# A hybrid decoder step in float32: which expert's down projection is kept in on-chip memory ahead of the weight stream, expert 7's or expert 31's

## The reference

```python
def hier_moe(t, w_route_group, w_route_expert, w_gate_up, w_down):
    ...
    out = jnp.zeros(t.shape, f32)
    for g in range(N_EXPERT_GROUPS):
        gu = jnp.einsum('td,edf->tef', t, w_gate_up[g])
        act = jax.nn.silu(gu[..., :D_EXPERT].astype(f32)) * gu[..., D_EXPERT:].astype(f32) * combine[:, g, :, None]
        out = out + jnp.einsum('tef,efd->td', act.astype(t.dtype), w_down[g], preferred_element_type=f32)
    return out.astype(t.dtype)
```

## Time and profile before

| | before |
|---|---|
| median of 3 runs | 1627.91 us (1625.69 to 1629.18) |
| the profiled execution's own time | 1627.91 us |
| its span (first to last instruction) | 1626.2 us |
| mean granted TensorE clock | 0.992 |
| TensorE matmul busy | 1579.4 us |
| moved by DMA | 542.22 MB, mean 333 GB/s |
| MoE of layer 0, from the first expert matmul to the end of the last down | 305.1 to 751.8 us |
| MoE of layer 1, the same | 1165.5 to 1611.7 us |

### The profile page before, as it was taken

The page is one execution under the profiler, slowest core; times in us unless marked ns, Lnnn a source line. Parts: engine busy times, 40 slices in busy tenths (PEclk is TensorE's granted clock), DMA queues, the critical chain, the costliest instruction groups (busy, mean ns, idle before and its releaser), DMA issues.

```text
span 1626.2 us, 20954 instructions
## 1 busy us (share of the span) xinstructions
PE 1579.4 (97%) x7891; PEld 903.4 (56%) x7891; DVE 604.9 (37%) x1360; ACT 448.7 (28%) x1168; POOL 128.5 (8%) x278
## 2 busy tenths in 40 slices
PE   9999899999999999999999999999999999999897
PEld 6877777543344344334877888877543444344342
DVE  4589983422222122224033454554421222122123
ACT  3488872211111111112143142232311111111112
POOL 1222231100000000001001202230000000000000
PEclk9999999999999999999999999999999999999999
DMA  9668776799999999999434947696799999999995
GB/s 343 209 217 247 257 239 277 261 393 423 426 426 426 429 425 427 429 424 395 160 140 144 341 167 246 176 274 282 287 395 421 428 428 425 428 429 425 426 427 218
DMA packets 108452, 542.22 MB, mean 333 GB/s; under 512 B 8876, under 2 KB 33652, under 8 KB 78642
## 3 DMA queue, kind: packets, MB, share of 16 engines
q1 hardware_dynamic: 91382, 485.20, 74.0%
q0 software_dynamic: 16672, 55.53, 10.7%
q10 hardware_dynamic: 316, 0.37, 0.1%
HBM read 524.81 MB, written 16.45 MB: 333 GB/s over the span
## 4 chain that ended last, share of the span: by engine, by line
PE 76%; DMA 12%; DVE 7%; ACT 4%; issue 1%; POOL 0%; SPq 0%; DVEq 0%; ACTq 0%; POOLq 0%
PE bank L1063 22%; PE bank L1437 14%; PE bank L1077 11%; DMA ring<-in_moe_w_gate_up 11%; PE bank L885 4%; PE bank L1071 4%; PE bank L1366 4%; PE bank L1339 3%; PE bank L1050 3%; PE bank L1666 2%; DVE arena L2339 1%; DVE arena L2494 1%; DMA arena<-scan_sums 1%; PE bank L1288 1%; PE bank L1092 1%
## 5 line engine op out<-in xcount | busy, mean ns | idle before, releaser
L1063 PE MATMUL bank<-ring,arena 128*64 128x512 f32 x1536 | 341.3, 600 | 14.7 <-DMA ring<-in_moe_w_gate_up 14.7
L1437 PE MATMUL bank<-hT,ring 128*128 128x264 f32 x1152 | 269.4, 389 | 0.2
L1063 PEld LDWEIGHTS bank<-ring,arena 128*64 128x64 f32 x1536 | 116.2, 138 | 232.8 <-issue 232.5
L1437 PEld LDWEIGHTS bank<-hT,ring 128*128 128x128 f32 x1152 | 214.3, 190 | 41.2 <-issue 3.9
L2339 DVE TENSOR_TENSOR arena<-arena,bank 128x512 f32<-128x512 f32 x32 | 34.3, 1071 | 409.2 <-ACT arena L1790 409.2
L1077 PE MATMUL bank<-ring,arena 128*64 128x512 f32 x768 | 170.1, 595 | 1.6 <-DVE arena L2257 1.6
L1071 PE MATMUL bank<-arena 128*128 128x512 f32 x256 | 126.9, 618 | 1.6 <-ACT arena L1800 1.6
L1790 ACT ACTIVATE arena<-bank 128x512 f32<-128x512 f32 x32 | 19.1, 597 | 395.4 <-PE bank L1063 395.4
L2283 DVE SCALAR_TENSOR_TENSOR arena<-arena 128x1024 f32<-128x1024 f32 x32 | 41.1, 1285 | 219.7 <-ACT arena L1800 219.7
L1063 PE MATMUL bank<-arena 128*64 128x512 f32 x512 | 112.8, 592 | 0.7 <-DMA arena<-in_moe_w_gate_up 0.7
L1077 PEld LDWEIGHTS bank<-ring,arena 128*64 128x64 f32 x768 | 53.9, 137 | 100.3 <-issue 97.5
(11 more groups left out here) (358 smaller groups left out, 1682.3 us busy)
## 6 DMA issues: line engine op xcount, KB each, us to landing
ring<-in_moe_w_gate_up SPq DMA_DIRECT2D x76, 2048.0 KB, 19.7
ring<-in_moe_w_down SPq DMA_DIRECT2D x44, 2048.0 KB, 24.5
arena<-in_moe_w_gate_up SPq DMA_DIRECT2D x32, 2048.0 KB, 20.5
ring<-in_moe_w_gate_up SPq DMA_DIRECT2D x40, 1024.0 KB, 17.3
ring<-in_attn_qkv SPq DMA_DIRECT2D x18, 2048.0 KB, 11.9
arena<-in_moe_w_down SPq DMA_DIRECT2D x28, 1024.0 KB, 23.8
ring<-in_ssm_in_proj SPq DMA_DIRECT2D x10, 2048.0 KB, 15.3
out<-arena POOLq DMA_DIRECT2D x24, 512.0 KB, 5.6
```

The costliest lines, as they stand in the source:

```text
L1063: mm = pe.matmul(bank[j][e * SLOTS:(e + 1) * SLOTS, :], Xg[:, 4 * half + k, 2 * (p % 2) + e, :], weights(2 * half + e, p)[:, k, j * DE:(j ...
L1437: mm = pe.matmul(bank[i % 2][:, 0:T], wv[:, k, (i % 4) * P:(i % 4 + 1) * P], hT[:, k, :], start=(n == 0), stop=(n == DT - 1))
```

## The change

The kept matrix becomes that of the last expert (`dn[NE - 1]`, expert 31, chunk 95) in place of expert 7's. Its two loads stay where they are on SP's queue, with the same waits. The stream now loads chunk 23, in halves together with chunk 22, and leaves chunk 95 out. TensorE's waits on the kept halves move from pair 3 to pair 15. Since the first turn no longer differs from the next two, the written-out copy of the first turn on SP goes, and the loop over q runs over three turns.

```diff
-                fixed = dn[DEEP - 1:DEEP].rearrange("o p n -> (o p) n")
+                last = dn[NE - 1:NE].rearrange("o p n -> (o p) n")
                 sp.wait_ge(s_oc, DT * (l + 1))
-                sp.dma_start(kept[1], fixed[:, CH // 2:CH]).then_inc(s_xld, 16)
+                sp.dma_start(kept[1], last[:, CH // 2:CH]).then_inc(s_xld, 16)
                 sp.wait_ge(s_ot, 8 * l + 6)
                 sp.wait_ge(m_ex, 3 * l + 1)
-                sp.dma_start(kept[0], fixed[:, 0:CH // 2]).then_inc(s_aux, 16)
+                sp.dma_start(kept[0], last[:, 0:CH // 2]).then_inc(s_aux, 16)
                 sp.wait_ge(m_R, l + 1)
                 more = sp.value_load(more_i[0:1, 0:1], min_val=0, max_val=ROUNDS - 1)
                 for c in EARLY_HALVED[::2]:
                     in_halves(c, 0, None)
-                def run(c0, c1, r, q, but=None):
-
-                    for c in range(c0, c1):
+                with sp.Fori(0, more + 1) as r:
+                    with sp.Fori(0, TURN - 1) as q:
+                        for c in range(DEEP + 4, DEEP + 28):
+                            if c % 24 < HALVED:
+                                chunk(c, r, q)
+                            elif c % 2 == 0:
+                                in_halves(c, r, q)
+                    for c in range(DEEP + 4 + 24 * (TURN - 1), 3 * NE):
                         if c % 24 < HALVED:
-                            chunk(c, r, q)
+                            chunk(c, r, None)
                         elif c % 2 == 0:
-                            in_halves(c, r, q, range(1 if c + 1 == but else 2))
-
-                run(DEEP + 4, DEEP + 28, 0, None, KEPT)
-                with sp.Fori(0, more + 1) as r:
-                    with sp.Fori(1, TURN - 1) as q:
-                        run(DEEP + 4, DEEP + 28, r, q)
-                    run(DEEP + 4 + 24 * (TURN - 1), 3 * NE, r, None)
+                            in_halves(c, r, None, range(2 if c + 2 < 3 * NE else 1))
                     with sp.If(r < more):
 
+                        in_halves(3 * NE - 2, r, None, (1,))
                         for c in range(3 * NE, 3 * NE + DEEP + 4):
                             chunk(c, r, None)
-                        run(3 * NE + DEEP + 4, 3 * NE + DEEP + 28, r, None)
...
-                        pe.wait_ge(deep[l], it * 96 + 32 * (turn + 1) - 16 * (kept_used or c >= KEPT - 1))
+                        pe.wait_ge(deep[l], it * 96 + 32 * (turn + 1) - 16 * (last and c >= 22))
...
-                        pe.wait_ge(done, it * 32 + base + (32 if first else 48 if j == 4 else 64))
+                        pe.wait_ge(done, it * 32 + base + (32 if first else 48 if last and j == 4 else 64))
...
-                    if not kept_used and 6 * p + j == KEPT - 1:
+                    if last and 6 * p + j == 22:
                         pe.wait_ge(s_aux, 64 + 16 * (l + 1))
                         pe.wait_ge(s_xld, 32 + 16 * (l + 1))
...
-                    if not kept_used and 6 * p + 4 + e == KEPT:
+                    if last and 6 * p + 4 + e == 23:
                         return kept[k // 2].rearrange("p (k n) -> p k n", k=2)[:, k % 2, :]
```

More of the change, by code:

```diff
@@ L1001, in token_counts, with chunk_landed @@
                               start=True, stop=True).then_inc(m_rk, 1)
-                def chunk_landed(j, it, p, kept_used):
+                def chunk_landed(j, it, p, last):
                     c = 6 * p + j
@@ L1012, in chunk_landed, with pair_landed, pair_begun @@
                     pe.wait_ge(loads[l][slot], it * 48 + 16 * (before + 1 + turn))
-                def pair_landed(j, it, p, kept_used):
-                    chunk_landed(j, it, p, kept_used)
-                    chunk_landed(j + 1, it, p, kept_used)
+                def pair_landed(j, it, p, last=False):
+                    chunk_landed(j, it, p, last)
+                    chunk_landed(j + 1, it, p, last)
                 def split(j, p, first):
                     return 6 * p + j >= HALVED or (first and 6 * p + j in EARLY_HALVED)
-                def pair_begun(j, it, p, first, kept_used):
+                def pair_begun(j, it, p, first=False, last=False):
                     if split(j, p, first):
                         done, base = firsts[l][j // 2 - 1]
-                        pe.wait_ge(done, it * 32 + base + (32 if first else 48 if j == 4 else 64))
+                        pe.wait_ge(done, it * 32 + base + (32 if first else 48 if last and j == 4 else 64))
                     else:
-                        pair_landed(j, it, p, kept_used)
-                    if not kept_used and 6 * p + j == KEPT - 1:
+                        pair_landed(j, it, p)
+                    if last and 6 * p + j == 22:
                         pe.wait_ge(s_aux, 64 + 16 * (l + 1))
@@ L1037, in weights, with down_rows @@
                     return w.rearrange("p (k n) -> p k n", k=4)
-                def down_rows(e, p, k, kept_used):
-                    if not kept_used and 6 * p + 4 + e == KEPT:
+                def down_rows(e, p, k, last):
+                    if last and 6 * p + 4 + e == 23:
                         return kept[k // 2].rearrange("p (k n) -> p k n", k=2)[:, k % 2, :]
@@ L1052, in gather, with gate_and_up @@
                     mm.then_inc(s.ga, 1)
-                def gate_and_up(half, it, p, first, kept_used):
-                    pair_begun(2 * half, it, p, first, kept_used)
+                def gate_and_up(half, it, p, first):
+                    pair_begun(2 * half, it, p, first)
                     for k in range(4):
                         if k == 2 and split(2 * half, p, first):
-                            pair_landed(2 * half, it, p, kept_used)
+                            pair_landed(2 * half, it, p)
                         for j in range(2):
@@ L1072, in scatter, with down @@
                               start=True, stop=True).then_inc(s.sc, 1)
-                def down(q, p, kept_used, ks=range(4)):
+                def down(q, p, last, ks=range(4)):
                     for k in ks:
@@ L1078, in down @@
                                            actT[:, k, e * SLOTS:(e + 1) * SLOTS],
-                                           down_rows(e, p, k, kept_used)[:, q * 512:(q + 1) * 512],
+                                           down_rows(e, p, k, last)[:, q * 512:(q + 1) * 512],
                                            start=(k == 0), stop=(k == 3))
@@ L1114, in moe, with four @@
                 pe.wait_ge(s_xa, 12 * l + 6)
-                def four(it, f, last=False, first=False, kept_used=True):
+                def four(it, f, last=False, first=False):
                     for h in range(2):
@@ L1124, in four @@
                         pe.wait_ge(s.cpt, it * 4 + p + 1)
-                        gate_and_up(0, it, p, first, kept_used)
+                        gate_and_up(0, it, p, first)
                         if nothing_yet:
@@ L1129, in four @@
                             pe.wait_ge(s.xg, it * 8 + 4 * f + 4)
-                        gate_and_up(1, it, p, first, kept_used)
+                        gate_and_up(1, it, p, first)
                         if nothing_yet:
@@ L1159, in four @@
                         pe.wait_ge(s.at, it * 4 + p + 2)
-                        pair_begun(4, it, p, first, kept_used)
+                        pair_begun(4, it, p, first, last)
                         if nothing_yet:
@@ L1163, in four @@
                         if not split(4, p, first):
-                            down(0, p, kept_used)
-                            down(1, p, kept_used)
-                        else:
[L1167 to L1174, removed]
+                            down(0, p, last)
+                            down(1, p, last)
+                        else:
+                            down(0, p, last, (0, 1))
+                            down(1, p, last, (0, 1))
+                            pair_landed(4, it, p, last)
+                            down(0, p, last, (2, 3))
+                            down(1, p, last, (2, 3))
+                four(0, 0, first=True)
+                four(0, 1)
                 pe.wait_ge(m_R, l + 1)
```

1 line of the change is left out of this document (removed).

## The result

The changed kernel takes 1638.2 us (median of 7 runs, 1634.55 to 1642.55) against 1627.91 us (7 runs, 1624.42 to 1631.12) for the kernel before: ratio 1.0061, 95% interval 1.0045 to 1.0078. The profiled execution took 1640.27 us, 2 us more than the median; its span is 1638.6 us. Before, the two are 1627.91 and 1626.2 us.

A forecast was written before the change was run, and what follows sets the result against it. TensorE bounds each MoE layer first, then the weight stream up to the wait at chunk 81. Two layers of 4.91 + 0.2 us give +10.2 us on 1627.91, so 1638.1 us; range 1632.5 to 1641.5.

The forecast's parts named there:

- The bound: Each MoE layer: TensorE sets the pace first, then the weight stream, 2.1 us per pair slower, until the wait at chunk 81.
- a lead of 20 us: At chunk 24 the stream was said to be 20 us ahead of TensorE, a lead eaten up by about pair 9.
- Chunk 23 joins: Chunks 24 to 94 land one chunk later, chunk 81 included, so each MoE layer ends 4.91 us later.
- rival A: Landings' lag vanishes or half speed stays out, absorbing part of the delay: 3.3 us a layer, 1634.5 us; chance 0.22.
- Chunk 95 leaves: End of each layer's stream: one load fewer gains 0, since nobody waits there.
- The kept halves: Loads keep place and size, and TensorE's waits move to pair 15, where they are long met: 0.
- The loop: First turn in the loop: chunk 12's later issue, at the stream's hole, delays the whole stream 0.2 us a layer.
- The clock: Half clock behind the wait ending at 676.52 costs 1.66 us when it comes; left as it is in the forecast.
- the prediction's signs: Wrong if a layer's last wait moves to another chunk with slack behind, DMA share drops below 1, or last down waits.
- B: Rival, no change: the delay ends before chunk 81 because TensorE would not be waiting there; 1627.9 us, chance 0.08.
- C: Rival, faster: earlier, spread waits keep the half clock away and the stream's delay stays below the refund; at most 1622.9 us, chance 0.05.
- D: Rival, slower still: one more half-clock stretch behind chunk 81 in each layer, +1.7 us each, 1641.5 us; chance 0.07.

The follow-up runs named there:

- run 3: Changed kernel with chunk 77 (expert 25, pair 12) as the kept matrix, chunks 23 and 95 streamed: 1626.49 us, ratio 0.9981 to the kernel before.
- run 4: Changed kernel with chunk 83 (expert 27, pair 13) as the kept matrix: 1637.44 us, ratio 1.0048 to the kernel before.
- run 1: Changed kernel with chunk 95 streamed and used too, the kept halves loaded but unused: 1638.95 us, ratio 1.0064 to the kernel before.
- run 6: Changed kernel with the first turn of 24 chunks written out on SP again: 1638.15 us, ratio 1.0048 to the kernel before.
- run 2: Kernel before with chunk 95 left out of the stream as well as chunk 23: 1629.32 us, ratio 1.0001.
- run 5: Kernel before with chunk 22 left out of the stream as well as chunk 23: 1626.36 us, ratio 0.9985.
- run 7: Kernel before with the second half of chunk 22 kept too, in free arena columns, everything computed: 1627.15 us, ratio 0.9987.
- run 8: Changed kernel with chunk 77 kept, chunk 76 left out of the stream, chunks 23 and 95 streamed: 1625.67 us, ratio 0.9979 to the kernel before.
- run 9: Changed kernel with chunk 77 and the second half of chunk 76 kept, everything computed: 1626.59 us, ratio 0.9988 to the kernel before.
- run 10: Kernel before with chunk 47 (expert 15, pair 7) as the kept matrix, chunks 23 and 95 streamed: 1628.52 us, ratio 0.9989.
- run 11: Kernel before with chunk 47 and the second half of chunk 46 kept, chunks 23 and 95 streamed, everything computed: 1621.91 us, ratio 0.9952.
- run 12: Kernel before with chunks 46 and 47 both left out of the stream, chunks 23 and 95 streamed: 1617.06 us, ratio 0.9912.

## Why the prediction was right

**The bound.** TensorE ahead at first, the stream slower by 2.1 us a pair, and the last wait at chunk 81: runs 3 and 4 show the last part from the time alone, with 11 us between a kept chunk just ahead of 81 and one just behind it. One sum of the prediction does not come out: a lead of 20 us, lost at 2.1 us a pair, lasts nearly ten pairs from pair 4 and not to pair 9. The lead that counts is that of chunk 27, the last of pair 4's second group: by the same rows it lands at 409.4 us and is wanted near 422.4, so it has 13 us, which lasts six pairs; the first wait before is at 558.7 us, in pair 9. The forecast did not use the sum.

**Chunk 23 joins: +4.91 us a layer.** Shown by run 1, which has this part and the loop alone and the whole of the loss, with run 6, which takes the loop away and keeps the loss, and by chunk 24's landing, later by 4.9 us. At chunk 81's group it measured +3.9 and +5.4 us in the changed kernel, and 3.5 to 5.2 in run 1. The scatter is that of the landings' lag, which I had put at 1.8 us: from chunk 24 to chunk 81 it is 680.0 - 399.6 = 280.4 us in layer 0 now against 281.7 before. So rival A's mechanism is real, 1.3 us of it in one layer of one execution. Chunk 91, counted in the same way, lands 4.6 and 5.4 us later than before, a mean of 5.0. By the medians the two layers cost 10.3 us, where 10.2 were forecast. That they agree to 0.1 us is luck: the interval of the ratio alone leaves 7.3 to 12.7 us.

**Chunk 95 leaves: 0.** Shown by run 1 and by run 2 (1.0001).

**The kept halves: 0.** TensorE's waits on them show in no row of pair 15. They were not tried apart.

**The loop: +0.2 us a layer.** The issue is late by 0.18 us, as read from the rows; the landing of chunk 12 in run 6 shows that its effect is not more than fractions of a us; the time alone bounds it to some 2 us. The term is unproven as a cost and too small to matter. The cover that the prediction gives to the loop's issues from chunk 24 on, some 3 us or more, is 0.6 us there by runs 5 and 7, which is still more than 0.18.

**The clock: left as it is.** Here the forecast was right by balance. The half clock came again behind chunk 81 in both layers, with one stretch in layer 0 and a double one in layer 1, where the group took 9.94 us (8.78 before) after a wait of 4.0 us (2.85 before). So of the 6.5 us of layer 1, 5.4 are the later start of chunk 81's group and 1.2 the clock, which the forecast had left out. Windows 679.6:683 and 1546.6:1553.4:

```profile
679.60:683.00 3.40, 2.90 (x8) 1.12 (x10) 0.00 (x0) 0.00 (x0) 0.00 (x0) 0.50 1.00 424
1546.60:1553.40 6.80, 5.79 (x14) 1.91 (x16) 0.00 (x0) 0.00 (x0) 0.00 (x0) 0.50 1.01 429
```

In run 6 the group ran at full clock in both layers (7.09 us). Layer 0 was not shorter than the changed kernel's for that: chunks 87 and 91 take the gain back, with waits of 1.6 and 0.7 us. Layer 1 was 2.3 us shorter, 0.6 of it by an earlier start of the group; there chunk 91 landed 1.8 us before the changed kernel wanted it, and so let most of the clock's gain through. In the changed kernel's own layer 0 chunk 91 also held TensorE for 0.3 us (729.83), so the 0.8 us of slack was used up there. That is one of the prediction's signs in part: the last wait for weights moved from chunk 81 to 91, though with no slack behind it.

**The rivals.** B fell with the result. C's condition never arose. D came in part, in one layer.

**What the profile was to show.** First wait near 532, in pair 8: 532.9. Waits of 13.7 and 12: 11.3 with the one at chunk 91, and 12.9. The 13.7 was too much, though layer 0 did grow by 4.2 us. Chunk 81 near 681.5: 680.0. The last landing near 745.5: 744.7 (issued at 718.2, 26.5 us to landing). Last down near 749.8: 748.5. An attention part as long as before: it was 2.1 us longer in the profiled execution. Its code is untouched, and over the other twelve runs it takes 413.8 to 416.6 us, so this lies within the scatter between executions. It explains why the spans differ by 12.4 us and the medians by 10.3.

**What I had wrong on the way** stands behind the prediction: that the price of a chunk would hold in both directions. Runs 5, 7, 8 and 9 corrected it, and runs 10 to 12 show what is left: a chunk counts in full if the queue stays full where it would stand, and if a wait of TensorE for weights still lies behind it.

## What to carry to other kernels

Where a stream of loads is slower than the engine that eats it, and the engine starts with a lead, on-chip space that is kept for one load is worth a load's time only if that load stands ahead of the engine's last wait; behind it the same bytes are worth nothing. It also has to stand behind the last point where loads are held up by places that are not free yet, or the time saved turns into an idle queue. Both edges can be read from one profile, the landing that ended the last wait and the DMA share in each stretch. The share alone does not show how much queue is spare: here it was 1.02 where only 0.6 us could be gained, and the time from issue to landing, 8.3 us against 7.7 with an empty queue, shows that. The edges have to be read again for each new version, since moving a load moves the waits.

## What was not expected of the hardware

After a TensorE wait of 2.7 us the granted clock falls to 0.50 in some cases and stays at 1.00 in others. In layer 0 of the changed kernel alone, the group of 32 matmuls at 650.72 took 7.09 us and that at 680.10 took 8.51 us, each after 2.70 us of idle time. In layer 1 of run 2 a group took 8.78 us after a wait of only 2.01 us. In layer 1 of the changed kernel the clock stayed at half for 6.8 us after a wait of 4.0 us, but the length does not follow the wait: in layer 1 of run 2 a group took 8.71 us after 4.26 us. In these runs each such stretch costs 1.3 to 3.0 us of TensorE's time. Where a wait for weights still follows in the layer, the next landing should take it up, though this was not tried apart; behind chunk 81 only chunk 91's landing can do that, as far as it is late enough.

The Trainium skill (TensorE: Matmul & The Clock Gate, "Why this matters for your kernels") asks for no long idle gaps between bursts of matmuls. The runs agree that a gap can bring the half clock: 8.51 us for a group after 2.70 us. What avoiding it gives is another matter: beside the changed kernel, run 6 had the full clock behind chunk 81 in both layers, and was 0.1 us shorter in layer 0 and 2.3 us in layer 1.
